# Separate step orders for three engines in the mixers of a transformer kernel, and matmuls without a reader

## The chip, the cores and the metric

The kernel runs on one core of a Trainium2 chip. The metric is the device time of one launch in microseconds. Three runs of the kernel before took 1310.43, 1317.64 and 1323.31 us; their median is 1317.64 us.

## The reference

The input is one sequence of 256 tokens with 1024 features, in float32. Two blocks follow each other. The first block has two layers. A layer is a gated feed-forward network (FFN, 2816 hidden features), the mixers, and a second FFN, each added to the running value:

```python
pa, pb, pc, pd = jnp.split(h @ w_in[l], IN_SPLITS, axis=-1)
ya = neighbourhood_mixer(pa, ...)   # 4 heads of 64, normed q and k, a bias table
yb = mla_mixer(pb, ...)             # latent q and kv, 4 heads of 64+32, rotation
yc = diff_mixer(pc, ...)            # 4 heads, difference of two softmaxes
yd = gqa_mixer(pd, ...)             # 4 query heads, 2 key heads, rotation
x = x + jnp.concatenate([ya, yb, yc, yd], axis=-1) @ w_out[l]
```

Each mixer is softmax attention over all 256 tokens (the neighbourhood one masks by a table), and its result is normalised before the product with `w_out`. The second block (one layer of three branches, and a projection) comes after both layers; the change does not touch it.

## The kernel before

Every large product is made of three matmuls in the fp32r type: a weight tile of 2048 columns is split on chip into a high and a low half (ScalarE writes `w_hi`, line 886; VectorE writes the rest `w_lo`, line 1197), and `product` (lines 441 to 445) multiplies high by high, low by high and high by low. The weights come through a ring of three slots of 1 MB. SyncE loads a slot when VectorE has split the one three places earlier; ScalarE and VectorE each split the slot two places ahead of the one that TensorE works on (`look_ahead`).

The tokens are in two tiles of 128. In the mixers the work of the engines is a list of steps, `ORDER`. All engines go through the same list, and each does its own part of a step:

- `proj` k: TensorE multiplies the input with 256 columns of `w_in` into one of two PSUM banks `pj`, ScalarE copies the bank out (line 1023) and both split a slot.
- `norm`, `prep`: ScalarE squares, VectorE sums, GpSimd takes the root (line 1713), VectorE scales (`prep`; for B and D also gains and the rotation). Norms and preps with the names yA to yD do this to the results of attention.
- `turn`, `latent`, `yturn`: TensorE transposes 128x128 blocks into one of two banks `tr` (line 597), and ScalarE, for `latent` and `yturn` VectorE too (line 1402), copies them out and frees the bank.
- attention goes in ten units, 0 to 9: units 0, 1 belong to mixer A, 2, 3, 6, 7 to C, 4, 5 to B, 8, 9 to D. A unit has `score` (TensorE line 607, fp32; VectorE finds the row maximum, line 1503 for B and D, line 1386 with the bias for A and C; ScalarE takes the exponential, line 1005), `soft` (VectorE: reciprocals, for C the difference, line 1522), `probs` (TensorE transposes, line 619; ScalarE copies, line 1015) and `pv` (TensorE line 627, fp32; VectorE writes the result, lines 1390, 1536, 1540).
- `wout` g: TensorE multiplies the turned result of mixer g with 256 rows of `w_out`.

Semaphores tie the steps. Those that matter below: `scores` of unit u waits until VectorE has written the result of unit u-2 (`y_set`), since both use the same half of the four banks `acc`; `begin_tr` waits until the bank of two fills before is free; `weigh` (`pv`) waits until ScalarE has copied both halves of `probs`; and the first `wout` waits for the results of all ten units. Within an engine everything is strictly in the order of the list, so a step that waits holds up whatever stands behind it.

The fills of the banks are numbered by `number(ORDER, ...)`, and the weight slots (`MIX_SLOTS`, `SLOT_OF`) by the order of `proj`, `latent_up` and `wout` in `ORDER`. In the late part of the list, after the last `proj`, TensorE has fp32 attention matmuls and transposes only, until the first `wout`.

Of the kernel before, what the change touches and what calls it, by code (L numbers as in the profile page):

```python
# [13 lines left out]
P = 128  # L14
S = 256
T = S // P
D = 1024
# [35 lines left out]

ORDER = [("proj", 0), ("proj", 1), ("norm", "A"), ("proj", 4), ("prep", "A"), ("proj", 3), ("norm", "latent"),
         ("turn", "A"), ("prep", "latent"), ("proj", 5), ("score", 0), ("score", 1), ("latent", 0),
         ("proj", 6), ("norm", "C"), ("soft", 0), ("soft", 1), ("proj", 2), ("probs", 0), ("latent_up", 0),
         ("prep", "C"), ("probs", 1), ("pv", 0), ("norm", "B"), ("turn", "C"), ("pv", 1), ("score", 2),
         ("score", 3), ("soft", 2), ("soft", 3), ("proj", 9), ("prep", "B"), ("proj", 7), ("probs", 2),
         ("norm", "yA"), ("proj", 8), ("probs", 3), ("pv", 2), ("turn", "B"), ("pv", 3), ("norm", "D"),
         ("score", 4), ("score", 5), ("prep", "D"), ("soft", 4), ("probs", 4), ("pv", 4), ("soft", 5),  # L60
         ("probs", 5), ("pv", 5), ("score", 6), ("score", 7), ("turn", "D"), ("soft", 6), ("soft", 7),
         ("probs", 6), ("prep", "yA"), ("norm", "yB"), ("probs", 7), ("pv", 6), ("pv", 7), ("norm", "yC"),
         ("yturn", "A"), ("score", 8), ("score", 9), ("soft", 8), ("prep", "yB"), ("prep", "yC"),
         ("soft", 9), ("probs", 8), ("probs", 9), ("pv", 8), ("pv", 9), ("yturn", "B"), ("norm", "yD"),
         ("prep", "yD"), ("yturn", "C"), ("wout", "A"), ("wout", "B"), ("yturn", "D"), ("wout", "C"),
         ("wout", "D")]

# [60 lines left out]
def build(nc, a):  # L128
    with ExitStack() as ctx:
# [160 lines left out]
        pj2, tr2, _, _ = number(ORDER2, pj_end, tr_end, pj_fills, tr_fills)  # L290
        PREP_SET = [s[1] for s in ORDER if s[0] == "prep" and s[1][0] != "y"]
        YNORM_SET = [s[1][1] for s in ORDER if s[0] == "prep" and s[1][0] == "y"]
        U = len(UNITS)
# [132 lines left out]
        def _(pe):  # L426
# [207 lines left out]
            def doubled():  # L634

                return [[k_twice[:, t, n * P:(n + 1) * P] for t in range(T)] for n in range(2)]

            def out_rows(wv, c0, first, last):

                for t, c in [(t, c) for t in range(T) for c in range(2)]:  # L640
                    for h in range(2):
                        ins = product(acc[:, 2 * t + h, :], hT(c0 + c, t * P, (t + 1) * P),
                                      wv(c, h * 512, (h + 1) * 512), first and c == 0, last and c == 1,
                                      begins=(c + t + h == 0))
                    if last and c == 1:
                        ins.then_inc(acc_full, 1)
# [10 lines left out]
            for l in range(L):  # L657
# [4 lines left out]
                for step in ORDER:  # L662
                    kind, k = step
                    if step == ORDER[0]:
                        proj_first(3 * l + 1, pj_[step], SLOT_OF[step], l)
# [211 lines left out]
        def _(act):  # L877
            def look_ahead(r, l, i=None):

                round_slot(r + 2, l, i)  # L880
# [158 lines left out]
            for l in range(L):  # L1039
# [10 lines left out]
                if l == 0:  # L1050
                    act.wait_ge(t5_out, 16)
                for step in ORDER:
                    kind, k = step
                    if kind == "proj":
                        c0, w = IN_BLOCKS[k]
                        look_ahead(SLOT_OF[step], l)
                        if step == ORDER[0]:
# [12 lines left out]
                    elif kind == "latent_up":  # L1070
                        look_ahead(UP_AT, l)
                        for j in range(4):
# [16 lines left out]
                    elif kind == "yturn":  # L1089
                        g = "ABCD".index(k)  # L1090
                        gain_out_y(l, tr_[step] - g, K_BETA, [g])
                    elif kind == "wout":
                        if step != ORDER[-1]:
                            look_ahead(SLOT_OF[step], l)
                    elif kind == "score":
# [79 lines left out]
        def _(dve):  # L1175
# [14 lines left out]
            def look_ahead(r, l, i=None):  # L1190

                rest_of_slot(r + 2, l, i)
# [232 lines left out]
            for l in range(L):  # L1425
# [14 lines left out]
                take_over(3 * l + 1, FFN1_AT + 34, l, 0.5)  # L1440
                for step in ORDER:
                    kind, k = step
                    if kind == "proj":
                        look_ahead(SLOT_OF[step], l)
                        if step == ORDER[0]:
                            means(3 * l + 1)
                    elif kind == "norm":
# [22 lines left out]
                    elif kind == "latent":  # L1470
                        for m in range(2):
# [8 lines left out]
                            ins.then_inc(tr_free[f % 2], 1)  # L1480
                    elif kind == "latent_up":
                        look_ahead(UP_AT, l)
                    elif kind == "score":
# [21 lines left out]
                    elif kind == "yturn":  # L1505
                        g = "ABCD".index(k)
                        gain_out_y(l, tr_[step] - g, K_BETA, [g])
                    elif kind == "wout":
                        if step != ORDER[-1]:
                            look_ahead(SLOT_OF[step], l)  # L1510
                    elif kind == "soft":
# [321 lines left out]
```

## Time and profile before

| | us |
|---|---|
| median of 3 runs | 1317.64 |
| the profiled execution | 1325.28 |
| span of its trace | 1323.0 |
| mixers of layer 0, first matmul to first matmul of the FFN after them | 197.7 to 348.2 |
| mixers of layer 1 | 718.7 to 867.0 |
[...]

The profiled execution is one run at the upper end of the three timed ones. The span starts with the first instruction. TensorE is called PE, VectorE DVE, ScalarE ACT in the rows. A matmul in fp32 has two rows of its own in the trace, a transpose one.

### The profile page before, as it was taken

To read this page: it belongs to the slowest core of one execution; us is meant where nothing else is said; L and a number is where in the kernel's file an instruction comes from. 1 tells how busy PE (TensorE), PEld (TensorE's weight loads), DVE (VectorE), ACT (ScalarE), POOL (GpSimd) and SP (SyncE) were. 2 spreads that over 40 slices of the span, in tenths; PEclk is the share of its full clock that TensorE was granted. 3 is DMA by queue.
4 is the path that set the end of the run, shared out by engine and by line. 5 is a ranking of instruction groups with operands and counts; after the bars stand their busy time and mean duration, and the time that the engine had idled before them with its cause. 6 is when DMAs were issued, how large, how long until landed. Compare 5 with 4: busy or idle time off the path is not lost.

```text
span 1323.0 us, 24755 instructions
## 1 busy us (share of the span) xinstructions
PE 1269.7 (96%) x10500; PEld 1243.6 (94%) x10500; DVE 841.3 (64%) x1059; ACT 640.1 (48%) x850; POOL 78.7 (6%) x57
## 2 busy tenths in 40 slices
PE   6999999988999999999999997999999999999997
PEld 6999999977999999999999996899999989899996
DVE  5766677775676666866657686576666754446665
ACT  4433356744443334533334774453333554666542
POOL 1111011210000000000001121000000000000000
PEclk9999999976999999999999996899999999999999
DMA  8786565320565555555565531246665655415542
GB/s 285 222 221 203 190 226 163 122 87 1 177 205 193 190 190 191 171 192 189 190 202 159 163 117 61 64 150 228 195 191 190 199 169 181 128 56 169 175 150 106
DMA packets 169515, 220.33 MB, mean 167 GB/s; under 512 B 5281, under 2 KB 152481, under 8 KB 169313
## 3 DMA queue, kind: packets, MB, share of 16 engines
q1 hardware_dynamic: 165680, 213.66, 50.1%
q0 software_dynamic: 2080, 2.48, 1.0%
q10 hardware_dynamic: 1680, 3.13, 0.7%
q8 instruction: 56, 0.92, 0.3%
q14 instruction: 19, 0.15, 0.0%
HBM read 218.15 MB, written 3.42 MB: 167 GB/s over the span
## 4 chain that ended last, share of the span: by engine, by line
PE 86%; ACT 6%; DVE 5%; issue 1%; DMA 1%; POOLq 0%; POOL 0%; DVEq 0%; ACTq 0%
PE pj L441 12%; PE pj L445 12%; PE pj L444 12%; PE acc L444 8%; PE acc L445 8%; PE acc L441 8%; PE tr L441 6%; PE tr L444 6%; PE tr L445 6%; PE acc L627 4%; ACT probs L1005 2%; ACT w_hi L886 1%; PE tr L619 1%; DVE w_lo L1197 1%; PE tr L597 1%
## 5 line engine op out<-in xcount | busy, mean ns | idle before, releaser
L1197 DVE TENSOR_TENSOR w_lo<-raw,w_hi 128x2048 fp32r<-128x2048 f32 (+2 forms) x206 | 458.8, 2228 | 242.7 <-ACT w_hi L886 241.3
L886 ACT ACTIVATE w_hi<-raw 128x2048 fp32r<-128x2048 f32 (+2 forms) x206 | 381.0, 1853 | 401.2 <-PE pj L441 142.7
L441 PE MATMUL pj<-hT_hi,w_hi 128*128 128x256 f32 x992 | 277.2, 279 | 2.6 <-DVE w_lo L1197 1.9
L445 PE MATMUL pj<-hT_hi,w_lo 128*128 128x256 f32 x992 | 275.7, 278 | 0.0
L444 PE MATMUL pj<-hT_lo,w_hi 128*128 128x256 f32 x992 | 275.6, 278 | 0.0
L445 PE MATMUL acc<-act_hi,w_lo 128*128 128x256 f32 x704 | 195.2, 277 | 0.0
L441 PE MATMUL acc<-act_hi,w_hi 128*128 128x256 f32 x704 | 195.2, 277 | 0.0
L444 PE MATMUL acc<-act_lo,w_hi 128*128 128x256 f32 x704 | 195.2, 277 | 0.0
L441 PEld LDWEIGHTS pj<-hT_hi,w_hi 128*128 128x128 f32 x992 | 187.2, 189 | 4.0 <-DVE w_lo L1197 2.1
L444 PEld LDWEIGHTS pj<-hT_lo,w_hi 128*128 128x128 f32 x992 | 186.7, 188 | 0.0
L445 PEld LDWEIGHTS pj<-hT_hi,w_lo 128*128 128x128 f32 x992 | 186.3, 188 | 0.0
L441 PE MATMUL tr<-hT_hi,w_hi 128*128 128x256 f32 x640 | 179.3, 280 | 1.8 <-DVE scratch L1302 1.8
L444 PE MATMUL tr<-hT_lo,w_hi 128*128 128x256 f32 x640 | 178.1, 278 | 0.0
L445 PE MATMUL tr<-hT_hi,w_lo 128*128 128x256 f32 x640 | 178.1, 278 | 0.0
L441 PEld LDWEIGHTS acc<-act_hi,w_hi 128*128 128x128 f32 x704 | 132.9, 189 | 0.0
L444 PEld LDWEIGHTS acc<-act_lo,w_hi 128*128 128x128 f32 x704 | 132.1, 188 | 0.0
L445 PEld LDWEIGHTS acc<-act_hi,w_lo 128*128 128x128 f32 x704 | 132.1, 188 | 0.0
L441 PE MATMUL pj<-w_hi,hT_hi 128*128 128x256 f32 (+1 forms) x448 | 126.6, 282 | 0.6 <-ACT proj L1023 0.6
L445 PE MATMUL pj<-w_hi,hT_lo 128*128 128x256 f32 (+1 forms) x448 | 124.7, 278 | 0.0
L444 PE MATMUL pj<-w_lo,hT_hi 128*128 128x256 f32 (+1 forms) x448 | 124.5, 278 | 0.0
L441 PEld LDWEIGHTS tr<-hT_hi,w_hi 128*128 128x128 f32 x640 | 121.4, 190 | 3.0 <-DVE scratch L1302 2.7
L444 PEld LDWEIGHTS tr<-hT_lo,w_hi 128*128 128x128 f32 x640 | 120.9, 189 | 0.3 <-issue 0.2
(212 smaller groups left out, 1991.7 us busy)
## 6 DMA issues: line engine op xcount, KB each, us to landing
raw<-in_w_in SPq DMA_DIRECT2D x47, 1024.0 KB, 5.3
raw<-in_ffn_w_up SPq DMA_DIRECT2D x44, 1024.0 KB, 5.4
raw<-in_ffn_w_down SPq DMA_DIRECT2D x44, 1024.0 KB, 5.0
raw<-in_ffn_w_gate SPq DMA_DIRECT2D x43, 1024.0 KB, 5.4
raw<-in_w_out SPq DMA_DIRECT2D x12, 1024.0 KB, 5.0
raw<-in_w_proj_a SPq DMA_DIRECT2D x4, 512.0 KB, 3.4
raw<-in_w_proj_b SPq DMA_DIRECT2D x4, 512.0 KB, 4.1
raw<-in_w_proj_c SPq DMA_DIRECT2D x4, 512.0 KB, 3.5
```

The lines of the kernel that those rows point to most:

```text
L441: ins = pe.matmul(out, lhs[0], rhs[0], start=first, stop=False, **kw)
L444: pe.matmul(out, lhs[0], rhs[1], start=False, stop=False, **kw)
L445: return pe.matmul(out, lhs[1], rhs[0], start=False, stop=last, **kw)
L597: ins = pe.transpose(bank[0:width, j, :], blocks[2 * m + j // 2][j % 2], ident)
L619: ins = pe.transpose(bank[:, j, :], probs[u % 2][:, h, kt * P:(kt + 1) * P], ident)
L627: ins = pe.matmul(ps[:, 0, h * 64:(h + 1) * 64], probsT[u % 2][:, h, kt, :], v(h, kt), start=(kt == 0), stop=(kt == nk - 1))
L886: act.activation(w_hi[r % RING][:, 0:w], raw[r % RING][:, 0:w], ACT.Copy).then_inc(hi_set, 1)
L1005: ins = act.activation(probs[u % 2][:, h, 0:nk * P], src[:, h, 0:nk * P], ACT.Exp, bias=smx[:, u % 2, h:h + 1], scale=scale, accum_out=ssu ...
L1197: dve.tensor_tensor(w_lo[r % RING][:, 0:w], raw[r % RING][:, 0:w], w_hi[r % RING][:, 0:w].bitcast(F32), ALU.subtract).then_inc(lo_set, 1)
```

## The change

`ORDER` becomes the order of TensorE alone, and ScalarE and VectorE get lists of their own, `ORDER_ACT` and `ORDER_DVE`, in which the split of a weight slot is a step of its own (`ahead`). The `norm` steps at the end of the new `ORDER` only number the roots of GpSimd, which keeps its order. What TensorE does in a step is unchanged. In the late part TensorE has now: score 4 ahead of pv 3; probs 5 ahead of probs 4; score 6 ahead of pv 5, score 7 behind it; the turn of yA between pv 6 and pv 7; that of yC ahead of pv 8; and the wouts in the order C, A, B, D in place of A, B, C, D.

Ahead of ten steps TensorE issues `keep_busy(n)`, matmuls of 256 columns from `br_hi` into the bank `pj[0]`, which nobody reads. The table `BUSY` gives their numbers: 10+10+6+3+20+15+10+10+6+3, which add up to 93 in the mixers of each layer (the short description of the change says 89). Ahead of the first of them TensorE waits for the last two fills of `pj` to be copied out.

```diff
+ORDER = [("proj", 0), ("proj", 1), ("proj", 3), ("proj", 4), ("turn", "A"), ("proj", 6), ("score", 0),
+         ("latent", 0), ("score", 1), ("proj", 5), ("proj", 2), ("probs", 0), ("latent_up", 0), ("probs", 1),
+         ("pv", 0), ("turn", "C"), ("pv", 1), ("score", 2), ("score", 3), ("proj", 8), ("proj", 7), ("probs", 2),
+         ("proj", 9), ("pv", 2), ("turn", "B"), ("probs", 3), ("score", 4), ("pv", 3), ("score", 5), ("probs", 5),
+         ("probs", 4), ("pv", 4), ("score", 6), ("pv", 5), ("score", 7), ("turn", "D"), ("probs", 6), ("probs", 7),
+         ("pv", 6), ("yturn", "A"), ("pv", 7), ("score", 8), ("score", 9), ("probs", 8), ("probs", 9),
+         ("yturn", "C"), ("pv", 8), ("pv", 9), ("yturn", "B"), ("wout", "C"), ("yturn", "D"), ("wout", "A"),
+         ("wout", "B"), ("wout", "D"), ("norm", "A"), ("norm", "latent"), ("norm", "C"), ("norm", "B"),
+         ("norm", "yA"), ("norm", "D"), ("norm", "yB"), ("norm", "yC"), ("norm", "yD")]
...
+ORDER_ACT = [
...
+             ("ahead", ("proj", 9)), ("norm", "yA"), ("probs", 2), ("proj", 7), ("proj", 9), ("turn", "B"),
+             ("norm", "D"), ("probs", 3), ("score", 4), ("score", 5), ("probs", 5), ("probs", 4), ("score", 6),
+             ("score", 7), ("turn", "D"), ("probs", 6), ("norm", "yB"), ("probs", 7), ("yturn", "A"),
+             ("norm", "yC"), ("score", 8), ("score", 9), ("probs", 8), ("probs", 9), ("yturn", "C"),
...
+ORDER_DVE = [
...
+             ("ahead", ("proj", 9)), ("norm", "D"), ("pv", 3), ("score", 4), ("score", 5), ("prep", "D"),
+             ("soft", 4), ("soft", 5), ("pv", 4), ("score", 6), ("pv", 5), ("score", 7), ("soft", 6), ("soft", 7),
+             ("prep", "yA"), ("norm", "yB"), ("pv", 6), ("pv", 7), ("score", 8), ("score", 9), ("norm", "yC"),
+             ("yturn", "A"), ("prep", "yC"), ("prep", "yB"), ("soft", 8), ("soft", 9), ("pv", 8), ("yturn", "C"),
+             ("pv", 9), ("norm", "yD"), ("prep", "yD"), ("yturn", "B"), ("yturn", "D"), ("ahead", ("wout", "C")),
...
+BUSY = {("probs", 3): 10, ("probs", 5): 10, ("pv", 4): 6, ("score", 6): 3, ("turn", "D"): 20, ("probs", 6): 15,
+        ("probs", 7): 10, ("pv", 6): 10, ("wout", "C"): 6, ("wout", "A"): 3}
...
+            def keep_busy(n):
+
+                for _ in range(n):
+                    pe.matmul(pj[0][:, 0, :], br_hi[:, 0, 0:P], br_hi[:, 1, :], start=True, stop=True)
...
+                    if step in BUSY:
+                        if step == next(iter(BUSY)):
+                            for f in (pj_stop[l] - 2, pj_stop[l] - 1):
+                                pe.wait_ge(pj_free[f % 2], f // 2 + 1)
+                        keep_busy(BUSY[step])
```

## Rows read from the trace of the kernel before

**Rows 1.** The page: span, TensorE's busy time, its clock in 40 slices.

```profile
span 1323.0 us, 24755 instructions
...
PE 1269.7 (96%) x10500; PEld 1243.6 (94%) x10500; DVE 841.3 (64%) x1059; ACT 640.1 (48%) x850; POOL 78.7 (6%) x57
...
PEclk9999999976999999999999996899999999999999
```

**Rows 2.** Busy times by stage; columns: stretch, length, PE, PEld, DVE, ACT, POOL, PEclk, DMA, GB/s.

```profile
197.70:220.50 22.80, 22.80 (x199) 22.80 (x198) 17.91 (x18) 13.12 (x16) 3.62 (x2) 1.00 0.56 167
...
271.00:282.00 11.00, 8.80 (x57) 7.11 (x55) 9.00 (x17) 8.01 (x26) 5.06 (x2) 1.00 0.56 192
282.00:324.20 42.20, 34.52 (x165) 30.89 (x165) 21.80 (x65) 16.81 (x55) 2.33 (x2) 0.59 0.00 1
324.20:348.20 24.00, 24.00 (x199) 24.00 (x198) 13.39 (x18) 12.38 (x18) 0.69 (x1) 0.94 0.43 132
...
718.70:741.20 22.50, 22.50 (x198) 22.50 (x197) 17.57 (x18) 13.03 (x16) 3.60 (x2) 1.00 0.56 170
...
803.00:842.70 39.70, 31.95 (x165) 28.15 (x165) 21.71 (x65) 16.61 (x55) 2.33 (x2) 0.61 0.00 1
842.70:867.00 24.30, 24.30 (x199) 24.30 (x198) 13.57 (x18) 12.55 (x19) 0.69 (x1) 0.93 0.43 131
```

**Rows 3.** The same view for short stretches of the late steps.

```profile
279.90:282.70 2.80, 0.66 (x4) 0.42 (x4) 2.66 (x5) 2.79 (x10) 0.00 (x0) 0.99 0.01 5
289.00:292.50 3.50, 3.50 (x16) 3.43 (x16) 0.00 (x0) 0.00 (x0) 0.00 (x0) 0.50 0.00 0
292.60:296.30 3.70, 3.70 (x22) 2.89 (x22) 1.89 (x8) 0.69 (x3) 0.00 (x0) 0.50 0.00 0
296.40:299.70 3.30, 0.43 (x4) 0.19 (x2) 3.07 (x13) 3.30 (x15) 0.00 (x0) 1.00 0.00 0
...
314.20:324.10 9.90, 9.90 (x47) 9.90 (x48) 1.47 (x4) 1.89 (x5) 0.00 (x0) 0.50 0.00 0
324.30:327.00 2.70, 2.70 (x15) 2.70 (x14) 1.47 (x4) 2.70 (x8) 0.69 (x1) 0.50 0.00 0
...
337.30:347.30 10.00, 10.00 (x91) 10.00 (x90) 5.48 (x8) 6.37 (x8) 0.00 (x0) 1.00 0.64 208
```

**Rows 4.** TensorE's instructions in order of time: start, length, line, count, idle before.

```profile
274.16 1.00 PE L627 MATMUL acc<-proj,probsT 128*128 128x64 f32 x8
275.06 3.69 PE L607 MATMUL acc<-qkT 96*128 96x256 f32 x16
...
288.97 3.65 PE L627 MATMUL acc<-up_buf,probsT 128*128 128x64 f32 x16 [0.78 <-ACT probsT L1015]
292.55 2.74 PE L607 MATMUL acc<-qkT 32*128 32x256 f32 x16
...
302.38 3.52 PE L627 MATMUL acc<-proj,probsT 128*128 128x64 f32 x16
305.69 1.06 PE L597 MATMUL tr<-const,hn 128*128 128x128 f32 x4
306.68 3.69 PE L607 MATMUL acc<-qkT 64*128 64x256 f32 x16
...
315.90 6.93 PE L627 MATMUL acc<-proj,probsT 128*128 128x64 f32 x32
```

**Rows 5.** VectorE's instructions in order of time, the same columns.

```profile
276.98 0.69 DVE L1503 TENSOR_REDUCE smx<-acc 128x2 f32<-128x512 f32 x1
...
280.70 0.96 DVE L1351 TENSOR_TENSOR proj<-proj,stat 128x768 f32<-128x768 f32 x1
...
287.69 0.42 DVE L1540 TENSOR_TENSOR hn<-acc,ssum 128x256 f32<-128x256 f32 x1
...
300.20 1.00 DVE L1522 SCALAR_TENSOR_TENSOR probs<-probs,ssum 128x256 f32<-128x256 f32 x2
...
308.79 0.69 DVE L1503 TENSOR_REDUCE smx<-acc 128x2 f32<-128x512 f32 x1
```

More of the change, by code:

```diff
@@ L49 @@
 I_ID, I_MC, I_MS, I_GC, I_GS, I_NA, I_MB, I_MM, NCONST = 0, 128, 192, 256, 384, 512, 576, 832, 1088
[L54 to L66, printed above, removed]
@@ new lines @@
+ORDER_DVE = [("means", 0), ("ahead", ("proj", 0)), ("ahead", ("proj", 1)), ("norm", "A"), ("ahead", ("proj", 3)),
+             ("prep", "A"), ("norm", "latent"), ("ahead", ("proj", 4)), ("prep", "latent"), ("score", 0),
+             ("score", 1), ("ahead", ("proj", 6)), ("latent", 0), ("soft", 0), ("norm", "C"),
+             ("ahead", ("proj", 5)), ("ahead", ("proj", 2)), ("ahead", ("latent_up", 0)), ("prep", "C"),
+             ("soft", 1), ("pv", 0), ("norm", "B"), ("pv", 1), ("score", 2), ("score", 3), ("soft", 2), ("soft", 3),
+             ("ahead", ("proj", 8)), ("prep", "B"), ("ahead", ("proj", 7)), ("norm", "yA"), ("pv", 2),
+             ("ahead", ("proj", 9)), ("norm", "D"), ("pv", 3), ("score", 4), ("score", 5), ("prep", "D"),
[3 more added lines that the diff above has]
+             ("pv", 9), ("norm", "yD"), ("prep", "yD"), ("yturn", "B"), ("yturn", "D"), ("ahead", ("wout", "C")),
+             ("ahead", ("wout", "A")), ("ahead", ("wout", "B"))]
@@ L290, in build @@
         pj2, tr2, _, _ = number(ORDER2, pj_end, tr_end, pj_fills, tr_fills)
-        PREP_SET = [s[1] for s in ORDER if s[0] == "prep" and s[1][0] != "y"]
-        YNORM_SET = [s[1][1] for s in ORDER if s[0] == "prep" and s[1][0] == "y"]
+        PREP_SET = [s[1] for s in ORDER_DVE if s[0] == "prep" and s[1][0] != "y"]
+        YNORM_SET = [s[1][1] for s in ORDER_DVE if s[0] == "prep" and s[1][0] == "y"]
         U = len(UNITS)
@@ L1051, in _ @@
                     act.wait_ge(t5_out, 16)
-                for step in ORDER:
+                for step in ORDER_ACT:
                     kind, k = step
+                    if kind == "ahead" and k != MIX_SLOTS[-1]:
+                        look_ahead(SLOT_OF[k], l)
                     if kind == "proj":
                         c0, w = IN_BLOCKS[k]
-                        look_ahead(SLOT_OF[step], l)
                         if step == ORDER[0]:
@@ L1070, in _ @@
                     elif kind == "latent_up":
-                        look_ahead(UP_AT, l)
                         for j in range(4):
@@ L1091, in _ @@
                         gain_out_y(l, tr_[step] - g, K_BETA, [g])
-                    elif kind == "wout":
-                        if step != ORDER[-1]:
-                            look_ahead(SLOT_OF[step], l)
                     elif kind == "score":
@@ L1440, in _ @@
                 take_over(3 * l + 1, FFN1_AT + 34, l, 0.5)
-                for step in ORDER:
+                for step in ORDER_DVE:
                     kind, k = step
[L1443 to L1446, printed above, removed]
+                    if kind == "ahead" and k != MIX_SLOTS[-1]:
+                        look_ahead(SLOT_OF[k], l)
+                    elif kind == "means":
+                        means(3 * l + 1)
                     elif kind == "norm":
@@ L1507, in _ @@
                         gain_out_y(l, tr_[step] - g, K_BETA, [g])
-                    elif kind == "wout":
-                        if step != ORDER[-1]:
-                            look_ahead(SLOT_OF[step], l)
                     elif kind == "soft":
```

10 lines of the change are left out of this document (8 added, 2 removed).

## The prediction, made before the changed kernel was run

> **What bounds the kernel now.** I read the page first: TensorE is busy for 96% of the span, so outside a few places nothing but its own work sets the time [rows 1]. The line of the clock shows the two exceptions, slices 8 and 9 and slices 25 and 26, and these are the late steps of the two mixers. Next I read the busy times by stage [rows 2]. [...] So a change here can win two things, the low clock and 7.7 us of idle in each, and it can lose by lengthening the chain of waits between score, maximum, exponential, transpose, pv and the next score.
>
> What the engine did before the clock moved is in [rows 3]. It fell at about 282.7, after a stretch of 2.8 us with 0.66 us of transposes. It came back at 296.3, after 3.7 us of unbroken scores of 256 columns and transposes, and fell again at 299.7, after 0.43 us of work in 3.3. From 314.2 to 324.1 TensorE was busy without a gap, with pv and transposes, and the clock stayed at 0.50; it came back at 327, some 3 us into the wide `wout` products. I reckon the new lists by their likeness to these stretches.
>
> **The prices.** A product of 256 columns costs 10.0/91 = 0.110 us at the high clock and 2.7/15 = 0.18 us in a stretch at the low one [rows 3]. A filler has the same shape and type; I take 0.114 us high and 0.228 us low, twice as much. 93 fillers are 10.6 us high, 21.2 us low. A pv of 16 records takes 3.5 us at the low clock (3.65 shown, its end modelled) [rows 4]; high I take half, 1.74. Scores of two units take 3.69 us for B at the high clock, for D at the low one; those of C 2.74 us [rows 4].
>
> **The walk.** I took the three new lists and let every step start when its engine is free and its waits are over, with durations from the trace, for the first mixers. The same walk over the old list puts the first `wout` at 322.9 (trace 324.2) and the end at 348.0 (348.2). Up to the last `proj` the new order changes nothing that I can see: TensorE goes from product to product, and the reordered projections, norms and slot splits stay behind them, as before [rows 2]. SyncE's queue sees the same number of loads; each slot is still split two places ahead, and the transfers stand still in the late part anyway. GpSimd keeps its order. The new wait for the copies of `pj` ahead of the first fillers costs nothing, as ScalarE copies that bank out ahead of turn B, which TensorE waits for already. Then:
>
> 1. Ten fillers (1.1), probs 3 (0.4) and both halves of score 4 (1.8) stand ahead of pv 3, which started at 274.16 [rows 4]. VectorE's list has the result of pv 3 ahead of the maximum of unit 4. That maximum starts at 279.0, against 276.98 [rows 5]: +2.0.
> 2. Four halves of maxima (3.7) and prep D (6.8, from 280.70 to the result of pv 4 at 287.69 [rows 5], with two small steps) are as long as before and still stand ahead of the result of pv 4, now at 289.9: +2.2. TensorE idles 1.9 us ahead of score 6 for it, and the six and the three fillers there do not fill that hole.
> 3. Old: pv 5 at 288.97, then score 6 and 7 in one piece [rows 4]. New: score 6 at 290.4, then pv 5, and score 7 must wait for VectorE's result of pv 5. After the hole I expect the low clock from about 289.5: score 6 1.7, pv 5 3.5, VectorE 0.7, so score 7 at 296.3. The maxima of unit 7 end at 299.1 against 298.0, soft 7 at 302.2 against 301.2 [rows 5]: +1.0.
> 4. TensorE meanwhile has 20 fillers (3.1, partly at the low clock), turn D (0.9), 15 fillers (1.7), probs 6 (0.4), ten (1.1), probs 7 (0.4), ten (1.1): pv 6 starts at 306.9, against 302.38 [rows 4]: +4.5. This is more than the gap holds; some 3 us of fillers lie on the path. But the clock is back, so pv 6, the turn of yA and pv 7 take 2.2 us in place of 4.3: score 8 at 309.1 against 306.68 [rows 4], +2.4. VectorE now does the maxima of units 8 and 9 first: 309.8 against 308.79 [rows 5], +1.0.
> 5. The bank `tr` that the turn of yA filled is freed by VectorE behind those maxima and norm yC (3.7+0.9+0.8), at 315.2. The second half of probs 8 needs this bank: a hole of 3 us on TensorE. Clock low again. Probs 9 and the turn of yC follow, and pv 8 starts at 318.8 against 315.90 [rows 4]: +2.9.
> 6. pv 8 and 9 (7.0 low, as 6.93 before [rows 4]), the turn of yB 0.9 (before two turns, 1.7, behind the pvs), six fillers at the low clock 1.4: first `wout` at 328.0 against 324.2: +3.8. Three more fillers and a slightly longer low stretch in `wout` bring the end to 352.6 against 348.2: **+4.4 us**.
>
> The second mixers took 148.3 us before (718.7 to 867.0), as the clock fell later there than in the first, which took 150.5 [rows 2]. The new lists give the same 154.9 us: **+6.6 us**. The sum is +11.0 us on the profiled execution's 1325.28, so 1336.3. That execution lies 7.6 us above the median of the runs; taken from the median of 1317.64 the forecast is **1328.6 us**.
>
> **The bounds.** Two prices are not in the trace: whether the clock holds over the new gaps, and what the mix of fillers and waits does to it. Upper bound on the gain: the clock high all through. The same walk then has score 7 at 293.7, pv 6 at 302.6, pv 8 at 313.3, the first `wout` at 317.9 and the end at 341.3: -6.9 and, for the second, -4.7 (148.3 less 143.6). Lower bound: low from 289 to the first `wout` in both; the 93 fillers then cost up to 21.2 us in place of 10.6, and the walk ends at 159: +8.5 and +10.7. I take +4.4 and +6.6, because the two holes of steps 2 and 5 are like those after which the clock fell [rows 3].
>
> **The rivals.** *The clock holds* (the other side). The place is the hole ahead of score 6: with fillers on both sides it might not cost the clock. For it: TensorE had 2.8 us with only 0.66 us of work before it fell [rows 3], and the new hole is 1.9 us, with nine fillers near. Against it: pv 4 stands beside it, stretches of pv ran at 0.50 without coming back [rows 3], and the second hole is 3 us. It decides where both holes leave the clock at 1.00: -11.6 us, 1306 us. If only the first one does, about -2 in each, 1313. Chance 0.22.
>
> [...]
>
> [...] Chance 0.20.
>
> *The reorder wins more than I see*: the lists were walked with fixed durations, and the exchange of yC and yA turns might take work off VectorE's path; then about no change, 1315 to 1320. Chance 0.10. That the change does nothing is out: 186 matmuls on an engine at 96% are seen.
>
> **The numbers.** Forecast 0.48: 1324 to 1334, likeliest 1329 us. The profiled execution's place among the runs moves everything by some 6 us. The range 1306 to 1342 takes in the clock-holds case and the fillers at the low clock. No change for a measurement here is within 1%, 13 us. My forecast of +11 lies just inside: of its 0.48, 0.20 falls beyond; of the low-clock rival nearly all, 0.18; in all slower 0.38. The clock-holds case at -11.6 us gives 0.10 beyond 1% and 0.12 within. Same is the rest, 0.52.
>
> **What would show it.** Step 1: the first maximum of unit 4 on VectorE 2 us later after the last `proj`. Step 2: an idle of about 2 us on TensorE ahead of score 6 (L607, 32 rows), put down to VectorE L1540. Step 3: the two C scores apart with a pv between. Step 4: pv 6 right behind ten fillers without idle. Step 5: an idle of 3 us between the two halves of probs 8, put down to L1402. The mean clock from the last `proj` to the first `wout` between 0.6 and 0.75; at 0.9 or more the first rival has won. I am wrong also if the part before the last `proj` is longer or shorter by over 1 us.

## The result, and the profile after

Four runs of the changed kernel took 1340.55, 1342.08, 1340.46 and 1325.56 us, median 1340.51; four of the kernel before on the same chip 1310.43 to 1325.62 us, median 1320.47. The ratio is 1.0144, with a 95% interval of 1.0083 to 1.0205. A repeat in more rounds (below) gave 1.0119, 1.0091 to 1.0147. **The change makes the kernel 1.2% slower**, some 16 us.

The first lines are from the page of the changed kernel: span, busy time of each engine with its instructions, the clock in 40 slices.

```profile
span 1338.3 us, 25127 instructions
...
PE 1286.3 (96%) x10686; PEld 1259.6 (94%) x10686; DVE 841.2 (63%) x1059; ACT 642.0 (48%) x850; POOL 92.7 (7%) x57
...
PEclk9999999987999999999999998799999999999999
```

The 186 matmuls are seen (10686 against 10500). The clock line looks better than before: 8 and 7, where [rows 1] has 7 and 6. GpSimd (POOL) has the same 57 instructions and is busy for 92.7 us, against 78.7 in [rows 1]; nothing in the change touches what it does. Next the busy times by stage of the changed kernel, for each layer's mixers: up to the end of the last `proj`, from there to the first `wout`, and the `wout` products. Columns as in [rows 2].

```profile
197.40:273.80 76.40, 73.24 (x611) 70.44 (x610) 54.54 (x93) 51.10 (x100) 22.40 (x6) 1.00 0.42 133
273.80:331.80 58.00, 49.61 (x316) 44.89 (x315) 31.97 (x83) 26.08 (x80) 5.29 (x4) 0.82 0.11 37
331.80:355.60 23.80, 23.80 (x201) 23.80 (x200) 12.49 (x16) 12.11 (x17) 0.70 (x1) 0.95 0.43 134
726.10:801.40 75.30, 72.17 (x611) 69.37 (x610) 54.14 (x93) 51.08 (x100) 22.16 (x6) 1.00 0.43 135
801.40:859.80 58.40, 50.27 (x316) 45.70 (x315) 32.36 (x83) 26.17 (x80) 5.29 (x4) 0.80 0.11 37
```

The mixers take 158.2 and 156.4 us, against 150.5 and 148.2: +15.9 us, and the spans differ by 15.3. So all of it is there. I split each at the end of the last `proj` (270.44 and 791.35 us in the kernel before). I call what lies ahead of that point the early part, and what lies behind it, `wout` included, the late part:

| | early | late |
|---|---|---|
| before | 72.7, 72.6 | 77.8, 75.6 |
| changed | 76.4, 75.2 | 81.9, 81.1 |

The late parts lose 4.1 and 5.5 us, as the forecast had it (4.4 and 6.6). The early parts lose 3.7 and 2.6 us, where it had nothing.

**The early part.** The same view of the kernel before has for the early parts:

```profile
197.70:270.44 72.74, 71.61 (x610) 69.97 (x609) 54.27 (x93) 50.92 (x100) 13.29 (x6) 1.00 0.45 140
718.70:791.35 72.65, 71.52 (x610) 69.89 (x609) 54.55 (x93) 50.72 (x100) 13.27 (x6) 1.00 0.45 140
```

TensorE was idle there for 1.1 us in each (length less busy time) and is idle for 3.2 and 3.1 us now: 2.0 us of the loss is waiting. The other 1.7 and 0.6 us are longer busy time for the same matmuls (610 and 611 records) at a granted clock of 1.00. I come back to this slower pace in the last section; its cause is open.

TensorE's timeline shows nearly all of the waiting as two holes in projections that had none before: 0.97 us ahead of the third projection and 0.89 us ahead of the turn of A.

```profile
210.28 0.38 PE L470 MATMUL pj<-w_hi,hT_hi 128*128 128x256 f32 x1 [0.97 <-ACT proj L1062]
...
222.41 1.09 PE L626 MATMUL tr<-const,proj 128*128 128x128 f32 x8 [0.89 <-DVE proj L1387]
```

ScalarE's copy of the first projection waits for the root of GpSimd (idle 4.69 us, put down to `xr`), and VectorE's scaling of A waits for another. GpSimd's timeline of the changed kernel gives both roots, and the one for the latent:

```profile
206.65 2.70 POOL L1719 TENSOR_TENSOR xr<-xr,half 128x2 f32<-128x2 f32 x1 [26.79 <-DVE xr L1286]
216.09 5.00 POOL L1744 TENSOR_TENSOR stat<-stat,half 128x16 f32<-128x16 f32 x1 [6.74 <-DVE stat L1224]
224.36 3.11 POOL L1744 TENSOR_TENSOR stat<-stat,half 128x4 f32<-128x4 f32 x1 [3.27 <-DVE stat L1224]
```

The same operations in the kernel before:

```profile
206.98 0.72 POOL L1688 TENSOR_TENSOR xr<-xr,half 128x2 f32<-128x2 f32 x1 [26.86 <-DVE xr L1250]
214.12 2.90 POOL L1713 TENSOR_TENSOR stat<-stat,half 128x16 f32<-128x16 f32 x1 [6.42 <-DVE stat L1188]
223.54 1.01 POOL L1713 TENSOR_TENSOR stat<-stat,half 128x4 f32<-128x4 f32 x1 [6.53 <-DVE stat L1188]
```

The changed kernel's take 2.0, 2.1 and 2.1 us more for the same elements. VectorE's timeline of the changed kernel says what it did meanwhile:

```profile
206.41 0.16 DVE L1286 TENSOR_SCALAR xr<-acc 128x2 f32<-128x2 f32 x1 [1.97 <-PE acc L499]
206.49 3.68 DVE L1233 TENSOR_TENSOR w_lo<-raw,w_hi 128x2048 fp32r<-128x2048 f32 x2
...
216.05 2.29 DVE L1233 TENSOR_TENSOR w_lo<-raw,w_hi 128x2048 fp32r<-128x2048 f32 x1
...
224.32 2.29 DVE L1233 TENSOR_TENSOR w_lo<-raw,w_hi 128x2048 fp32r<-128x2048 f32 x1
```

In each of the three cases the split of a weight slot began 0.04 to 0.16 us ahead of the GpSimd operation and took 2.29 us (a split of 2048 columns; the first row holds a second, shorter split too). In the kernel before a split stood beside the root of A as well, but it began 0.04 us *behind* it, and the root took its 2.90 us:

```profile
214.16 2.32 DVE L1197 TENSOR_TENSOR w_lo<-raw,w_hi 128x2048 fp32r<-128x2048 f32 x1
```

Further on the root for C takes 6.73 us for 5.42 and the copy behind it 2.01 for 0.39, while the root of yA, which took 2.80 us at 271.46 in the kernel before, takes only 0.70. The balance is +7.0 us in each layer's mixers, which is the whole of 92.7 less 78.7.

**The late part.** TensorE's timeline of the changed kernel, in the first mixers:

```profile
293.16 1.89 PE L636 MATMUL acc<-qkT 32*128 32x256 f32 x8 [1.47 <-DVE hn L1571]
294.98 3.68 PE L656 MATMUL acc<-up_buf,probsT 128*128 128x64 f32 x16
299.24 2.08 PE L636 MATMUL acc<-qkT 32*128 32x256 f32 x8 [0.58 <-DVE hn L1571]
...
310.73 1.00 PE L656 MATMUL acc<-proj,probsT 128*128 128x64 f32 x8
...
316.18 0.66 PE L648 MATMUL tr<-const,probs 128*128 128x128 f32 x4 [1.14 <-ACT probs L1044]
319.84 1.13 PE L648 MATMUL tr<-const,probs 128*128 128x128 f32 x8 [3.00 <-DVE hT_lo L1438]
...
322.98 6.93 PE L656 MATMUL acc<-proj,probsT 128*128 128x64 f32 x32
```

Score 6 waits 1.47 us, pv 5 behind it takes 3.68 us, at a granted clock of 0.50 (1.00 is full speed); pv 6 stands right behind ten fillers; the second half of probs 8 waits 3.00 us; and pv 8 and 9 take 6.93 us, at 0.50 again. The clock in short stretches of the same timeline:

```profile
289.30:291.60 2.30, 2.30 (x19) 2.18 (x19) 2.13 (x6) 0.00 (x0) 0.00 (x0) 1.00 0.00 0
291.60:293.10 1.50, 0.08 (x1) 0.00 (x0) 1.27 (x5) 0.00 (x0) 0.00 (x0) 1.00 0.00 0
295.00:298.60 3.60, 3.60 (x17) 3.46 (x16) 1.55 (x8) 2.08 (x8) 0.00 (x0) 0.50 0.00 0
305.60:313.00 7.40, 7.40 (x68) 7.33 (x65) 1.96 (x6) 3.81 (x12) 0.69 (x1) 1.00 0.00 0
316.90:319.80 2.90, 0.00 (x0) 0.00 (x0) 2.62 (x7) 2.50 (x11) 0.93 (x1) 1.00 0.00 0
323.00:329.60 6.60, 6.60 (x33) 6.60 (x33) 1.30 (x3) 0.84 (x2) 0.00 (x0) 0.50 0.00 0
```

The clock falls behind each of the two holes and comes back between them, during the 20 fillers ahead of turn D (3.70 us for them; the mean is 0.50 from 301.20 to 303.00 and 0.88 from there to 305.60, so part of them ran at the low clock). The second mixers repeat the pattern (1.47 us ahead of score 6, 3.01 us inside probs 8).

### The profile page after: what moved, and what is told of

The parts are those of the page before. It is cut to its first block and busy times, and to the rows that moved or that the text cites. A ratio compares the mean times of both kernels' runs of the same rounds, so it can differ in the third digit from the quotient of the medians.

```text
span 1338.3 us, 25127 instructions
## 1 busy us (share of the span) xinstructions
PE 1286.3 (96%) x10686; PEld 1259.6 (94%) x10686; DVE 841.2 (63%) x1059; ACT 642.0 (48%) x850; POOL 92.7 (7%) x57
```

## The experiments

Twelve kernels were run. Early and late are the two parts of each mixer in the profiled execution; the ratio to the kernel before comes from the timed runs.

| kernel | early | late | ratio, 95% interval |
|---|---|---|---|
| change, repeated | 75.6, 76.4 | 82.5, 77.7 | 1.0119, 1.0091 to 1.0147 |
| new orders, no fillers | 76.0, 76.4 | 76.5, 78.6 | 1.0086, 1.0051 to 1.0120 |
| old orders, fillers | 73.1, 73.1 | 79.5, 82.6 | 1.0033, 1.0011 to 1.0056 |
| old early, new late and fillers | 73.1, 72.2 | 80.2, 80.9 | 1.0064, 1.0037 to 1.0091 |
| new early, old late | 76.0, 76.4 | 70.5, 76.3 | 1.0037, 0.9991 to 1.0084 |
| ScalarE exchange | 78.1, 76.9 | 77.4, 82.5 | 1.0162, 1.0118 to 1.0205 |
| tiny operations ahead of splits | 73.9, 73.5 | 76.0, 82.3 | 1.0046, 1.0015 to 1.0076 |
| fillers in the two holes | 75.5, 76.4 | 74.6, 72.8 | 1.0009, 0.9981 to 1.0037 |
| bank freed early | 76.0, 76.4 | 80.4, 80.3 | 1.0103, 1.0071 to 1.0135 |
| own orders, no fillers | 72.8, 72.7 | 66.4, 66.4 | 0.9876, 0.9845 to 0.9906 |
| own orders, 60 fillers | 72.8, 72.8 | 62.2, 62.2 | 0.9819, 0.9780 to 0.9859 |
| the same, fillers out | 72.7, 72.7 | 68.8, 67.5 | 0.9904, 0.9878 to 0.9930 |

Two things are to be read from the table before any single row. The early part is fairly stable: 72.2 to 73.1 us with the old lists, 75.2 to 76.4 with the new ones as they are. The late part is not: one and the same set of late lists gave 76.0 to 82.5 us in ten stretches, since the clock comes and goes at other points from one execution to the next: its mean from the last `proj` to the first `wout` was 0.87 in the shortest of the ten and 0.77 in the two longest. So an early edit of over 1 us can be judged by one profile; for a late one I go by the ratios. Each ratio is to runs of the kernel before in the same session. The change's repeat, the edits and the own orders come from several sessions, so a difference of two ratios carries the errors of both.

**The repeat.**

> The changed kernel once more, unaltered, in more rounds, since every comparison with it rests on four runs of which one (1325.56 us) stands 15 us below the other three. If the usual time is near 1340 us, the ratio to the kernel before stays at 1.014 and a second profile has the two mixers at some 314 us together. If the low run is as common as the others, the ratio falls to about 1.010 and the difference lies in the late parts, where the clock falls at another place. The early parts are the same in both cases: 75 to 77 us, with the GpSimd operation at 2.70 us.

It took 1332.53 us (1331.87 to 1335.74, six runs) against 1319.14. The usual time lies between the three first runs at 1340 to 1342 us and the fourth at 1325.56, the ratio is 1.0119, and the early parts and the root (2.70 us) are as expected.

**The parts of the change, one by one.** The new orders alone:

```diff
-BUSY = {("probs", 3): 10, ("probs", 5): 10, ("pv", 4): 6, ...
+BUSY = {}
```

> The changed kernel with its three new orders and an empty table of fillers. My theory: the 89 matmuls (10.6 us at the high clock, partly in the waits) lie on the path with about 4 us in each mixer's late steps, so this kernel is some 8 us faster than the changed one and 6 to 10 us slower than the kernel before (3.7 and 2.6 us of it in the part up to the last `proj`, which the fillers do not touch; the late part 0 to 3 us longer in each). The mean clock from the last `proj` to the first `wout` falls back from 0.82 to about 0.7. Rival, the fillers earn what they cost through the clock: the time stays within 2 us of the changed kernel's. Rival, the orders alone are neutral: the time is that of the kernel before.

1327.36 against 1318.86 us, 1.0086, or 11 us, just beyond the 6 to 10 expected. Without the fillers the clock between last `proj` and first `wout` is 0.68 in both mixers, as expected, but the time is less than with them: 0.33% lies between this ratio and that of the repeat, about 4 us, where 8 were expected (the intervals overlap). By this pair alone that is no more than a hint that the fillers do not pay for themselves; the next run shows it. The second rival, neutral orders, is out.

The fillers alone, ahead of the same ten steps of the old order:

```diff
-ORDER = [("proj", 0), ("proj", 1), ("norm", "A"), ("proj", 4), ...
+ORDER, ORDER_ACT, ORDER_DVE   # the old order, written as three lists
+BUSY = {("probs", 3): 10, ("probs", 5): 10, ("pv", 4): 6, ...
```

> The orders of the kernel before, written as three lists, with the fillers ahead of the same ten steps as in the change. My theory: nothing changes up to the last `proj` (within 0.3 us), the fillers cost 4 to 6 us in each mixer, in all +8 to +12 us against the kernel before. Rival, the fillers keep the clock and pay for themselves: 0 or below. Rival, they lie in the waits: 0, with the same clock as before.

1324.84 us, 1.0033, 4.4 us, with the whole interval above 1. The sign is as expected, the size is half of it: my price for the fillers with these orders was too high, though this profile's mixers are 9.7 us longer than those of the profile before. The fillers raise the clock from last `proj` to first `wout` here too, from 0.68 and 0.70 in the kernel before to 0.82 and 0.78, and still lose.

Old lists up to the last `proj`, new ones behind it, with the fillers:

```diff
 ORDER_DVE = [
-             ("means", 0), ("ahead", ("proj", 0)), ("ahead", ("proj", 1)), ("norm", "A"), ...
+             ("ahead", ("proj", 0)), ("means", 0), ("ahead", ("proj", 1)), ("norm", "A"), ...
 # and so on to the last proj, in all three lists
```

> The changed kernel's late orders and fillers, but all three lists up to the last `proj` as in the kernel before. My theory: the part from the start of a mixer to the end of the last `proj` is back at 72.8 us (76.6 and 75.4 in the changed kernel), the rest stays as in the changed kernel: 6 us faster than it, +9 to +11 us against the kernel before. Rival, the early loss only moves a wait that the late part would have had anyway: the time stays at the changed kernel's, within 2 us.

The early part is back (73.1 and 72.2 us), GpSimd is busy for 78.7 us, and the ratio of 1.0064 is 0.55% below the repeat's, 7 us; 6 were expected. Against the kernel before it is +8.4 us, a little under the 9 to 11 expected.

The reverse, new lists up to the last `proj` only, no fillers:

```diff
-  ("proj", 9), ("pv", 2), ("turn", "B"), ("probs", 3), ("score", 4), ("pv", 3), ("score", 5), ("probs", 5), ...
+  ("proj", 9), ("probs", 3), ("pv", 2), ("turn", "B"), ("pv", 3), ("score", 4), ("score", 5), ("probs", 4), ...
+BUSY = {}
```

> The reverse: all three lists as in the change up to the last `proj`, behind it the orders of the kernel before, no fillers. My theory: +6 us against the kernel before, all of it in the early part, with GpSimd's operations on the rows of the residual stream taking 2.7 and 5.0 us (0.73 and 2.9 before) beside VectorE's splits. Rival (what the prediction said), the early part is free: within 1 us of the kernel before.

The early part is 76.0 and 76.4 us, with GpSimd busy for 92.9 us: +3.3 and +3.7, 7 us in all where 6 were expected, and what the prediction said of it is refuted. The ratio, 1.0037 (about 5 us), agrees, but its interval reaches below 1: its ten runs spread from 1313 to 1338 us, and its first late part happened to take 70.5 us.

Split by the ratios, the loss of 1.19% is 0.37% for the early part, 0.49% for the new late orders (the row without fillers less the early part) and 0.33% for the fillers. The middle share is a difference, so that these add up tests one thing only: the fillers cost the same alone as beside the new orders. Taken from the other side the early part is worth 0.55%. The intervals of these kernels are 0.2 to 0.5% to either side, so the shares are rough. Well measured are the early part, by the profiles, and that the fillers alone lose.

**Why GpSimd is slow.** Two attempts. First the exchange in ScalarE's list:

```diff
 ORDER_ACT = [
-             ("ahead", ("proj", 0)), ("ahead", ("proj", 1)), ("proj", 0), ...
+             ("ahead", ("proj", 0)), ("proj", 0), ("ahead", ("proj", 1)), ...
```

> The changed kernel with one exchange in ScalarE's list: the copy of proj 0 stands ahead of the look-ahead for proj 1, as in the kernel before, so that VectorE's second split comes later. Theory, GpSimd is slowed by VectorE's splits beside it: its first operation on the residual (2.70 us in the changed kernel) is back near 0.73 us and the idle of 0.97 us ahead of the third projection is gone: 1 to 2 us less in each mixer, -2 to -4 us against the changed kernel. Rival, only the order of ScalarE's list matters and GpSimd's length is a symptom: GpSimd's operation stays at 2.7 us, and the time falls all the same. Rival, neither: within 1 us of the changed kernel.

A miss: the root stayed at 2.70 us, the hole of 0.97 us too, the one ahead of the turn of A grew to 1.60 us, and the early parts are 1.7 us longer than in the changed kernel's profile (in the first of them the clock fell for 3.4 us as well). I had moved the wrong split. VectorE's timeline of this kernel shows the first one still right behind the means, and only the second one later:

```profile
205.79 0.16 DVE L1283 TENSOR_SCALAR xr<-acc 128x2 f32<-128x2 f32 x1 [1.96 <-PE acc L496]
205.87 2.28 DVE L1230 TENSOR_TENSOR w_lo<-raw,w_hi 128x2048 fp32r<-128x2048 f32 x1
210.80 1.49 DVE L1230 TENSOR_TENSOR w_lo<-raw,w_hi 128x1280 fp32r<-128x1280 f32 x1 [2.65 <-ACT w_hi L922]
```

So I left the order alone and only delayed the splits by one small operation, so that GpSimd starts first:

```diff
-                for step in ORDER_DVE:
+                for n_, step in enumerate(ORDER_DVE):
                     kind, k = step
+                    if kind == "ahead" and ORDER_DVE[n_ - 1][0] in ("means", "norm"):
+                        step_(dve.tensor_scalar(lam[:, 0:1], lam[:, 0:1], 1.0, None, ALU.mult))
```

> The changed kernel with one tiny operation (128x1) more on VectorE between each norm (or the means) and the look-ahead behind it, four in each mixer, so that GpSimd's power starts before VectorE's split does. Theory: a GpSimd operation that starts while a split (w_lo) runs stands until the split ends; one that started first is not slowed. Then the four powers take 0.73, 2.9, 1.0 and 5.4 us in place of 2.70, 5.00, 3.11 and 6.73, the early part falls from 76.4 and 75.2 to about 73.5 us, and the time by 4 to 6 us against the changed kernel. Rival, GpSimd is slow for another reason (the exchange of ScalarE's list left it at 2.70): its durations stay, the time too. Rival, the durations fall but the early part does not, as the projections wait for ScalarE's look-aheads: within 1 us.

GpSimd's timeline of this kernel:

```profile
206.52 0.72 POOL L1721 TENSOR_TENSOR xr<-xr,half 128x2 f32<-128x2 f32 x1 [26.82 <-DVE xr L1286]
214.79 2.90 POOL L1746 TENSOR_TENSOR stat<-stat,half 128x16 f32<-128x16 f32 x1 [7.55 <-DVE stat L1224]
222.86 1.01 POOL L1746 TENSOR_TENSOR stat<-stat,half 128x4 f32<-128x4 f32 x1 [5.17 <-DVE stat L1224]
238.79 5.42 POOL L1746 TENSOR_TENSOR stat<-stat,half 128x32 f32<-128x32 f32 x1 [14.93 <-DVE stat L1224]
```

and VectorE beside the first two:

```profile
206.35 0.14 DVE L1480 TENSOR_SCALAR lam<-lam 128x1 f32<-128x1 f32 x1
206.53 3.72 DVE L1233 TENSOR_TENSOR w_lo<-raw,w_hi 128x2048 fp32r<-128x2048 f32 x2
...
214.93 2.29 DVE L1233 TENSOR_TENSOR w_lo<-raw,w_hi 128x2048 fp32r<-128x2048 f32 x1
```

All four durations are the expected ones, to 0.02 us, although the splits still run beside the roots. They now begin 0.01 and 0.14 us behind them. The holes of 0.97 and 0.89 us are gone, the early parts are 73.9 and 73.5 us (TensorE idle for 1.3 us in each, 3.2 and 3.1 before this edit), and GpSimd is busy for 74.5 us. The ratio fell to 1.0046; against the repeat that is 0.7%, 10 us, of which the early parts explain 4.5. The rest is in the late parts, where it can be the place at which the clock fell; I have not shown that.

The durations of the roots that started behind a split agree within 0.2 us with a sum: such a root takes its own time and what is left of the split (0.72 + 2.29 - 0.16 = 2.85 for 2.70; 2.90 + 2.25 = 5.15 for 5.00; 1.01 + 2.25 = 3.26 for 3.11). For a split that started behind a root there is no such sum: the one that began 0.14 us into a root of 2.90 us (the last row above) took 2.29 us, as elsewhere, and ended before the root did, and the one at 214.16 in the kernel before took 2.32. So in these traces GpSimd stands for VectorE's split, and the split does not stand for the root.

**The two holes.** The changed kernel, with fillers where it waits:

```diff
-        ("score", 6): 3, ...
+        ("score", 6): 16, ...
+                    if u in (8, 18) and m == 0:    # between the halves of probs 8
+                        keep_busy(24)
```

> The changed kernel with more fillers in its two holes: 16 in place of 3 ahead of score 6, and 24 between the two halves of the transposes of unit 8. If these two holes are what loses the clock, then it stays at 1.00 from the last `proj` to the first `wout` (0.82 in the changed kernel), pv 5 and pv 8 and 9 take 1.8 and 3.5 us in place of 3.7 and 6.9, and each mixer is 5 to 7 us shorter: -10 to -14 us against the changed kernel. If the clock falls for another reason (the pv stretches themselves), the 37 fillers only add: +2 to +8 us. Between the two: the clock is held through the first hole alone, about -3 us in each.

TensorE's timeline around the second hole:

```profile
313.67 3.13 PE L669 MATMUL pj<-act_hi 128*128 128x256 f32 x24
316.93 1.06 PE L645 MATMUL tr<-const,probs 128*128 128x128 f32 x8
...
319.28 3.68 PE L655 MATMUL acc<-proj,probsT 128*128 128x64 f32 x32
```

pv 8 and 9 take 3.68 us in place of 6.93, pv 5 2.00 in place of 3.68, and the clock between last `proj` and first `wout` is 0.93 and 0.97. Not quite 1.00: in the first mixers it falls with score 7, and the 20 fillers behind that take 4.64 us:

```profile
295.60:302.40 6.80, 6.80 (x33) 6.08 (x30) 4.84 (x19) 2.23 (x10) 0.00 (x0) 0.50 0.00 0
```

The ratio is 1.0009, 1.1% or 14.5 us below the repeat's (10 to 14 were expected), for 74 more matmuls. So the two holes are where most of the low clock comes from. They are not all of it: with both filled the clock still fell, for 6.8 us here and for 3.4 us in the second mixers, behind pv 5 and a wait of 0.59 us ahead of score 7. Which of these two brought it down no run separates.

**Is the hole the bank's?** Step 5 blamed the bank that VectorE frees late. Here it is freed first:

```diff
-             ("pv", 7), ("score", 8), ("score", 9), ("norm", "yC"), ("yturn", "A"), ...
+             ("pv", 7), ("yturn", "A"), ("score", 8), ("score", 9), ("norm", "yC"), ...
```

> The changed kernel with VectorE's result of the turn of yA moved ahead of the maxima of units 8 and 9, so that the bank of the transposes is free at once. By step 5 of the prediction, read alone, the hole of 3.0 us between the halves of probs 8 goes and pv 8 starts 2 to 3 us earlier: -4 to -6 us. By the walk of waits with the new list, the hole goes but the maxima and with them the exponentials come 0.9 us later and the next wait takes its place: 0 to -1 us in each mixer. Against both: the idle between the halves stays at 3.0 us, then the named releaser was not the cause.

The idle put down to the bank is gone, and another has taken its place, as the walk had it. The transposes of units 8 and 9 in this kernel:

```profile
315.73 0.66 PE L648 MATMUL tr<-const,probs 128*128 128x128 f32 x4 [1.19 <-ACT probs L1044]
316.66 0.66 PE L648 MATMUL tr<-const,probs 128*128 128x128 f32 x4 [0.27 <-ACT probs L1044]
319.09 1.94 PE L648 MATMUL tr<-const,probs 128*128 128x128 f32 x8 [1.78 <-ACT probsT L1054]
```

The second half comes 2.7 us earlier (counted from the last `proj`), but probs 9 then waits 1.78 us for ScalarE, whose copies stand behind the exponentials of unit 9. Pv 8 starts 48.7 us behind the last `proj` (49.2 in the changed kernel), and still takes 6.93 us. The ratio, 1.0103, is 0.16% below the repeat's, within the error.

**Orders of my own.** With the walk that gave the forecast I looked for late orders in which, with fillers, no wait is long. Up to the last `proj` TensorE's list is that of the kernel before, and those of ScalarE and VectorE differ from it in a few steps just ahead of that point; behind it:

```diff
 ORDER (TensorE):
+  ..., ("pv", 3), ("score", 4), ("score", 5), ("probs", 4), ("probs", 5), ("pv", 4), ("pv", 5),
+  ("score", 6), ("score", 7), ("turn", "D"), ("probs", 6), ("probs", 7), ("pv", 6), ("pv", 7),
+  ("score", 8), ("score", 9), ("probs", 8), ("pv", 8), ("probs", 9), ("yturn", "A"), ("pv", 9),
+  ("yturn", "C"), ("yturn", "B"), ("wout", "A"), ("wout", "B"), ("yturn", "D"), ...
 ORDER_DVE:
+  ..., ("score", 5), ("prep", "D"), ("soft", 4), ("pv", 4), ("soft", 5), ("pv", 5), ("score", 6),
+  ("score", 7), ("soft", 6), ("soft", 7), ("norm", "yB"), ("pv", 6), ("prep", "yA"), ("pv", 7),
+  ("score", 8), ("norm", "yC"), ("soft", 8), ("score", 9), ("prep", "yC"), ("prep", "yB"),
+  ("soft", 9), ("pv", 8), ("yturn", "A"), ("pv", 9), ...
+BUSY = {("probs", 4): 3, ("probs", 5): 15, ("score", 6): 6, ("turn", "D"): 10, ("probs", 6): 20,
+        ("pv", 8): 6}
```

The turn of yA stands behind the transposes of unit 8, so that it holds no bank that they want, and score 6 stands behind both pv 4 and 5.

> A version of my own: early lists as in the kernel before; in the late steps the turns of the output stand behind the scores and transposes of the last units, so that no bank is held, and VectorE takes each prep and norm where TensorE does not wait for it; 60 fillers ahead of six steps. By the walk that gave the forecast, with the clock high all through, a mixer takes 134 us against 149 in the kernel before: -25 to -30 us, clock from the last `proj` to the first `wout` at 0.95 or more. Rival, the walk of waits misses what it did for the change (work beside work that slows both): -10 to -15 us. Rival, the clock falls anyway: 0 to -8 us.

1291.48 us, three of four runs between 1289.99 and 1291.57 (the fourth took 2538.2 us; why is not known, and the comparison leaves it out). The mixers take 134.95 us each, where the walk had 134. The ratio, 0.9819, against 1313.71 us for the kernel before in the same session, is 22 to 24 us, some less than the 25 to 30 expected, as the kernel before was at its quick end there. By the profiles the two mixers together are 28.8 us shorter, inside the expected range. The spans differ by 33.9; the other 4.9 us are a slower pace of TensorE between the mixers in the profile of the kernel before (last section), and not the orders' doing. By stage, from last `proj` to first `wout`:

```profile
270.30:310.20 39.90, 36.05 (x286) 32.53 (x285) 32.34 (x85) 25.12 (x79) 7.40 (x4) 1.00 0.09 27
770.90:810.80 39.90, 35.97 (x287) 32.54 (x285) 32.30 (x85) 25.12 (x79) 7.40 (x4) 1.00 0.09 28
```

The clock never falls; the stretch takes 39.9 us where it took 53.7 and 51.3. The same without its fillers:

```diff
-BUSY = {("probs", 4): 3, ("probs", 5): 15, ("score", 6): 6, ...
+BUSY = {}
```

> My faster version with fillers (1291 us), without its 60 fillers. If fillers pay where the orders leave short gaps, the clock falls without them: by the walk 136 to 144 us per mixer in place of 134.95, +2 to +18 us, likeliest +14. Rival, the orders alone do it: the same time, or up to 2 us less.

```profile
270.40:316.90 46.50, 38.18 (x227) 33.33 (x225) 32.35 (x85) 25.33 (x79) 7.40 (x4) 0.74 0.08 23
```

0.9904, 1303.72 us; the mixers take 141.5 and 140.2 us, near the middle of the expected range. TensorE's longest waits in its first mixers are 1.78 us ahead of probs 5 and 3.09 us ahead of probs 6, the places where 15 and 30 of the fillers stood (10 of the 30 ahead of turn D); with the fillers none was over 1.14 us. So here 60 fillers bring 0.85%, 11 us, where 93 cost 0.33% in the change. And orders looked for with no fillers at all, which differ from those above mainly in:

```diff
-  ("probs", 4), ("probs", 5), ("pv", 4), ("pv", 5), ...
+  ("probs", 4), ("pv", 4), ("probs", 5), ("pv", 5), ...
-  ("probs", 8), ("pv", 8), ("probs", 9), ("yturn", "A"), ("pv", 9), ("yturn", "C"), ("yturn", "B"), ...
+  ("probs", 8), ("yturn", "A"), ("pv", 8), ("probs", 9), ("yturn", "B"), ("pv", 9), ("yturn", "C"), ...
+BUSY = {}
```

> Similar orders of my own, chosen with no fillers at all: early lists as before, late turns of the output behind the scores. By the walk 138 us per mixer: -18 to -22 us against the kernel before. Tells whether fillers are needed at all. Rival, without fillers the clock falls in the waits as before: 0 to -8 us.

0.9876, 1298.40 us, with mixers of 139.1 us (the walk had 138), at a clock of 0.80. In time that is 15 to 16 us, under the 18 to 22 expected; the mixers of the profiles are 20.5 us shorter together. About two thirds of the gain over the kernel before needs no filler.

## Why the prediction was right and where it was wrong

The forecast, 1329 us, is 11 us below the median of the changed kernel and 4 us below the repeat's; the range holds both. On the profiled executions +11.0 us was forecast and +15.3 measured. The direction was right, but "slower by over 1%" deserved more than "within 1%".

*The step that failed* is the sentence "Up to the last `proj` the new order changes nothing that I can see". It cost 3.7 and 2.6 us. I compared the order of the steps and the number of loads, and saw that GpSimd keeps its order; I did not ask what VectorE does at the moment at which GpSimd starts. By the sign that the prediction itself names, an early part longer by over 1 us, it was wrong there. The list of VectorE puts a split directly behind the means, behind norm A, behind norm latent and behind norm C. Where the split started ahead of the root, the root stood until it ended (2.70 us for 0.72, 5.00 for 2.90, 3.11 for 1.01, 6.73 for 5.42). The small operations ahead of the splits took that away, and with it 2.5 and 1.7 us of the 3.7 and 2.6. Of this 1.9 and 1.8 us are waits of TensorE that went; what is left, 1.2 and 0.9 us, is mostly its slower pace at a clock of 1.00, which nothing here explains.

*Steps 1 to 6* held in this execution, measured from the end of the last `proj` (3.34 us later in the changed kernel, subtracted here). First maximum of unit 4: 278.3, forecast 279.0, so 1.4 us later than in [rows 5] and not 2.0. Result of pv 4: 289.3, forecast 289.9, the hole ahead of score 6 1.47 us for 1.9. Score 7: 295.9 for 296.3. Pv 6: 307.4 for 306.9. Second half of probs 8: 316.5, a hole of 3.0 us for 3. Pv 8: 319.6 for 318.8. First `wout`: 328.5 for 328.0, end 352.3 for 352.6. In the second mixers the late part lost 5.5 us for 6.6. The sum of both late parts is +9.6, forecast +11.0; with the early 6.3 it is 15.9. That single steps agree to 0.3 to 0.8 us shows that the walk has the right waits; that the late sum agrees so well is partly luck, as the same late lists took from 76.0 to 82.5 us in other stretches.

*Step 5* was right in what it saw and incomplete as a cause: the bank's wait is the last of two that end close together. With the bank free (1.0103) nearly all of the loss stays.

*The mean clock* was to be 0.6 to 0.75 from last `proj` to first `wout`; it was 0.82 and 0.80. That range did not follow from my own walk: it has the clock low from 289.5 to about 299 and from about 316 to 328, some 21 of 57.5 us, which is a mean of 0.81. The clock line rose and the time rose with it, since the raised clock ran over fillers.

*The price of the fillers.* I put their net cost at some 3 us in each mixer and let them bring the clock back for pv 6 and 7. The runs give 0.33% for all of them, 4.4 us, over both mixers, alone and with the new orders alike. The late orders themselves cost about as much (0.49%); the walk did not part the two.

*The first rival*, the clock holds, did not happen, but its mechanism is real: where the two holes are filled (1.0009) or absent (0.9819) the clock holds at 0.93 to 1.00. Fillers elsewhere do not make up for them (0.82 and 0.80 in the changed kernel), and the clock also fell behind a wait of only 0.59 us. *The fillers at the low clock*, the rival with the chance of 0.20, happened in part. No run shows the case that the prediction's numbers reckon with, all the fillers of step 4 at 0.50: of the 20 ahead of turn D those of the second mixers took 4.6 us and those of the first 3.70, and the 15 behind them 2.0 us in both.

## What to carry to other kernels

Fill or remove the wait itself: matmuls without a reader paid where they filled the two waits of 1.5 and 3 us of the changed kernel (1.1% against its repeat) or where they stood in the waits of 1.8 and 3.1 us of the own orders (0.85%), and lost (0.33%) where waits of 1.5 to 3 us stayed open beside them. The own orders were also steadier, 1.6 to 2.0 us between the runs of each, against 17 us over 23 runs of the kernel before. This is not a matter of holding the clock: two of the three had it at 0.74 to 0.80 in the late part, and the kernel with filled holes, at 0.93 and 0.97, spread over 8.6 us. What makes the difference is not shown. Between a small operation of VectorE that releases GpSimd and a long one like the `w_lo` split of 2.29 us behind it, let GpSimd start first; 0.2 us decided over 2 us.

## What the runs showed of the hardware

A GpSimd operation that starts inside a VectorE `w_lo` split of 2.29 us shows the wait as its own duration: 0.72 became 2.70, 2.90 became 5.00, 1.01 became 3.11 us. One that starts 0.01 or 0.14 us ahead of the split is not slowed (0.72 and 2.90 us), and neither is the split behind it (2.29 and 2.32 us for splits that began 0.14 and 0.04 us behind a root). The profile counts this wait as busy time and names no releaser for it; a group's busy time that grows with the same count is the sign (78.7 to 92.7 us for GpSimd's 57 instructions).

TensorE had a second, slightly slower pace at a granted clock of 1.00. Between the two mixers, where no kernel differs, the same matmuls took 370.5 us in three of the fourteen profiles (the kernel before and the changed one among them) and 365.6 to 367.2 in the others. Stretches of the changed kernel, and of the one with own orders and fillers, at the same place of the program:

```profile
627.40:726.10 98.70, 98.70 (x840) 98.70 (x839) 61.45 (x57) 38.93 (x30) 3.50 (x1) 1.00 0.59 186
```

```profile
604.30:698.10 93.80, 93.80 (x830) 93.80 (x829) 60.93 (x57) 38.93 (x29) 3.52 (x1) 1.00 0.61 194
```

4.9 us apart with the clock at 1.00 and no idle in either. One thing goes with it: in the eleven quicker profiles the granted clock had fallen to 0.50 for 3.4 us (6.8 in the kernel with filled holes) at the change of layers, 173 to 176 us ahead of the second mixers, and in the three slower ones it had stayed at 1.00. The slower pace begins at that place. That is a coincidence in fourteen profiles and no cause shown. The early parts differ too at a clock of 1.00, and that is part of the early loss above: the twelve with the new lists and no edit to them have TensorE busy for 72.2 to 73.3 us, the twelve with the old ones or close to them for 71.2 to 72.1. Whether that is the same pace is not shown.
